# First block's output projection inside the mixer's last steps, and the gate of the linear attention on ScalarE

## What is computed

```python
def _gla_output(o, g, norm_g):
    ...                                     # o: linear attention, normalised per head
    return (...).astype(o.dtype) * jax.nn.silu(g)

def _trunk_layer(x, cvec, lp, ctx, pos):
    sh1, sc1, gt1, sh2, sc2, gt2 = jnp.split(jax.nn.silu(cvec) @ w_ada + b_ada, 6, axis=-1)
    h = _rmsnorm(x, n1) * (1 + sc1) + sh1
    ...                                     # h @ w_in, split among three mixers: pool, GLA, attention
    mix = jnp.concatenate([y_pool, y_gla, y_attn], axis=-1)
    x = x + gt1 * (mix @ w_out)             # output projection, gated residual
    h2 = _rmsnorm(x, n2) * (1 + sc2) + sh2
    x = x + gt2 * _peer(h2, peer_wq, peer_subkeys, peer_u, peer_v)
```

## Time and profile before

| | us |
|---|---|
| median of 3 runs | 4006.52 |
| the profiled execution's own time | 3995.5 |
| its span, first to last instruction | 3993.7 |
| TensorE busy | 3697.8 |
| VectorE busy | 2609.3 |
| GpSimd busy | 1616.5 |
| ScalarE busy | 680.5 |
| mean granted clock of TensorE | 0.961 |

### The profile page before, as it was taken

The page is one execution under the profiler, slowest core; times in us unless marked ns, Lnnn a source line. Parts: engine busy times, 40 slices in busy tenths (PEclk is TensorE's granted clock), DMA queues, the critical chain, the costliest instruction groups (busy, mean ns, idle before and its releaser), DMA issues. The chain is left out here.

```text
span 3993.7 us, 40043 instructions
## 1 busy us (share of the span) xinstructions
PE 3697.8 (93%) x13766; PEld 2139.0 (54%) x13766; DVE 2609.3 (65%) x5973; ACT 680.5 (17%) x1534; POOL 1616.5 (40%) x1498
## 2 busy tenths in 40 slices
PE   2988978999999999999979888889999999999997
PEld 1556676655555555554445666766555555555543
DVE  5786588776666666677724738978677646566444
ACT  1031356500000000000012224652000000000000
POOL 0030055445566544444402002553677655444330
PEclk7987999999999999999989799999999999999998
DMA  6321134579999999999930131447899999989783
GB/s 222 122 95 50 74 96 138 158 291 406 374 380 374 377 372 378 376 377 355 372 129 2 44 117 38 133 138 254 340 410 410 390 364 344 367 338 359 290 308 130
DMA packets 364809, 1026.96 MB, mean 257 GB/s; under 512 B 30784, under 2 KB 132416, under 8 KB 363840
## 3 DMA queue, kind: packets, MB, share of 16 engines
q0 software_dynamic: 147456, 536.94, 35.1%
q1 hardware_dynamic: 117424, 433.99, 28.5%
q10 hardware_dynamic: 99728, 53.48, 4.8%
HBM read 965.07 MB, written 59.22 MB: 256 GB/s over the span
## 5 line engine op out<-in xcount | busy, mean ns | idle before, releaser
L1835 PE MATMUL ps<-colsT,arena 128*128 128x384 f32 x4096 | 1358.7, 486 | 4.2 <-DMA arena<-in_peer_ut 4.2
L1835 PEld LDWEIGHTS ps<-colsT,arena 128*128 128x128 f32 x4096 | 775.9, 190 | 582.6 <-issue 94.7
L1870 PE MATMUL ps<-arena 128*128 128x512 f32 x1536 | 676.4, 592 | 0.0
L1349 POOL DMA_INDIRECT proj<-in_peer_u,eidx x336 | 460.0, 1369 | 244.0 <-DVE modbc L1541 116.1
L1349 POOL DMA_INDIRECT proj<-in_peer_v,eidx x335 | 359.5, 1073 | 315.7 <-DVE colsT L1552 216.9
L1870 PEld LDWEIGHTS ps<-arena 128*128 128x128 f32 x1536 | 291.8, 190 | 345.2 <-issue 317.6
L1335 POOL TENSOR_SCALAR x<-iota,modbc 128x128 f32<-128x128 f32 x192 | 145.0, 770 | 759.9 <-ACT modbc L1672 593.0
L1541 DVE CUSTOM_DVE_ANT_0 proj<-proj,rows 128x1024 f32<-128x1024 f32 x336 | 400.4, 1224 | 56.3 <-DMA proj<-in_peer_u,eidx 54.6
L1552 DVE SCALAR_TENSOR_TENSOR colsT<-proj,modbc,colsT 128x1024 f32<-128x1024 f32 x330 | 409.6, 1285 | 14.9 <-DMA proj<-in_peer_v,eidx 14.7
L1870 PE MATMUL ps<-arena,rows 128*128 128x512 f32 x768 | 337.8, 592 | 0.0
L1870 PE MATMUL ps<-arena,x 128*128 128x512 f32 x768 | 337.8, 592 | 0.0
(11 more groups left out here) (295 smaller groups left out, 3775.2 us busy)
## 6 DMA issues: line engine op xcount, KB each, us to landing
arena<-in_peer_ut SPq DMA_DIRECT2D x256, 512.0 KB, 6.7
arena<-in_peer_v SPq DMA_DIRECT2D x256, 512.0 KB, 6.7
gmat_d<-arena ACTq DMA_DIRECT2D x24, 2048.0 KB, 9.3
arena<-gmat_d SPq DMA_DIRECT2D x64, 768.0 KB, 8.7
proj<-in_w_adaT SPq DMA_DIRECT2D x48, 512.0 KB, 9.2
modbc<-in_w_adaT SPq DMA_DIRECT2D x30, 512.0 KB, 3.7
rows<-in_w_adaT SPq DMA_DIRECT2D x18, 512.0 KB, 3.5
arena<-in_w_in SPq DMA_DIRECT2D x2, 4224.0 KB, 17.4
```

The costliest lines, as they stand in the source:

```text
L1349: pool.indirect_dma_start(ring[slots[at]], None, tab, bass.IndirectOffsetOnAxis(ap=eidx[:, b * SLOTS + q:b * SLOTS + q + 1], axis=0)).then ...
L1835: mm = pe.matmul(ps[:, 2 + j % 2, 0:ND], utab[:, j % UR, k], hT[:, k, NG:T], start=(k == 0), stop=(k == KT - 1))
L1870: mm = pe.matmul(ps[:, Y_BANKS[2 * d + c2], :], wT[j % CR][:, d * P:(d + 1) * P], vtab[:, j % VR, c2 * 512:(c2 + 1) * 512], start=(j == 0) ...
```

## The change

Four things, in both layers.

1. The gate. ScalarE now makes the whole of 1/(1+exp(-g)) in step 11, as exp(-ln(1+exp(-g))): three passes over 128x1280 (Exp, Ln, Exp). VectorE's add and reciprocal of step 12 are gone, and its wait for `sg_ready` stands in step 13.
2. The projection. `out_proj(0)` moves into the mixer block as `first_projection`: its first half stands in step 21 behind `turn_y(18)`, its second in step 22 behind `turn_y(19)`. It writes PSUM banks 6 and 7 in place of 0 and 1. The first half waits for w_out, for the copies of `gt1` on ScalarE and VectorE, and for the attention output of its token block.
3. The gate row. The first DMA of the second block is the latents' gate row alone (0.5 MB, to `loaded`). SP waits for it to land before it issues `w_q`; behind `w_q` stand the prompt's gate row (0.5 MB) and shift and scale for both kinds (2 MB), which only the residuals of blocks 0 and 1 wait for (`rows_landed`).
4. `residual(0)` waits for no matmul of the second block, since the barrier stands between; `residual(i)` waits for `wo_mm` at i.

```diff
--- before.py
+++ after.py
@@ -191,8 +191,7 @@
         sem("av_done"), sem("y_made"), sem("yt_done"), sem("yt_sb"), sem("es_ready"), sem("gs_half"), sem("gs_done"))
     go_done, P_ready, gla_ready, gm_ready, gy_ready, sg_ready, pool_d = (
         sem("go_done"), sem("P_ready"), sem("gla_ready"), sem("gm_ready"), sem("gy_ready"), sem("sg_ready"), sem("pool_d"))
-    wq_landed = (
-        sem("wq_landed"))
+    wq_landed, rows_landed = sem("wq_landed"), sem("rows_landed")
     sc_half, ms_made, root_made = sem("sc_half"), sem("ms_made"), sem("root_made")
     dots_ready, gelu_ready, coef_ready = sem("dots_ready"), sem("gelu_ready"), sem("coef_ready")
 
@@ -766,6 +765,18 @@
                         turn_mod()
                     else:
                         turn_gla(n)
+
+                def first_projection(n):
+                    if n == 0:
+                        pe.wait_ge(wo_landed, 16)
+                        pe.wait_ge(u_act, ACT_AT["gt1"])
+                        pe.wait_ge(u_dve, DVE_AT["gt1"])
+                        pe.wait_ge(y_moved, 1)
+                        pe.wait_ge(yt_sb, pairs_.index((3, DB[0])) + 1)
+                    b = DB[0]
+                    for k in range(KT):
+                        pe.matmul(ps[:, 6 + n, :], mixT[:, k, b * P:(b + 1) * P], w_out[:, k, n * 512:(n + 1) * 512],
+                                  start=(k == 0), stop=(k == KT - 1))
 
                 if l > 0:
                     turn_normed(pe)
@@ -814,6 +825,8 @@
                         state_mm(2)
                     if SC0_STEP <= s < SC0_STEP + NB:
                         chunk_out(s - SC0_STEP)
+                    if s >= PSTEPS - 2:
+                        first_projection(s - PSTEPS + 2)
 
             @block.scalar
             def _(act):
@@ -891,8 +904,10 @@
                         act.wait_ge(yt_sb, NB)
                         act.activation(mixT[:, 4, :], ytmp, ACT.Copy).then_inc(y_moved, 1)
                     if s == 11:
-                        act.activation(sg.rearrange("p b c -> p (b c)"), gg.rearrange("p b c -> p (b c)"), ACT.Exp,
-                                       scale=-1.0).then_inc(sg_ready, 1)
+                        flat = lambda q: q.rearrange("p b c -> p (b c)")
+                        c.link(act.activation(flat(sg), flat(gg), ACT.Exp, scale=-1.0))
+                        c.link(act.activation(flat(sg), flat(sg), ACT.Ln, bias=1.0))
+                        act.activation(flat(sg), flat(sg), ACT.Exp, scale=-1.0).then_inc(sg_ready, 1)
                     if s == OUT_STEP:
                         act_rstd(act, c, None, gm_ready, gy_ready, msg, yg, zg)
 
@@ -1059,11 +1074,8 @@
                             c.done(dve.tensor_tensor(v(arr)[:, :, 32:64], v(arr)[:, :, 32:64], v(right)[:, :, 32:64], ALU.mult))
                         c.wait()
                         dve.sem_inc(qk_ready, 1)
-                    if s == 12:
+                    if s == 13:
                         dve.wait_ge(sg_ready, 1)
-                        c.link(dve.tensor_scalar(f(sg), f(sg), 1.0, None, ALU.add))
-                        c.link(dve.reciprocal(f(sg), f(sg)))
-                    if s == 13:
                         c.link(dve.tensor_tensor(f(sg), f(sg), f(gg), ALU.mult))
                         c.link(dve.tensor_tensor(sg, sg, gnorm.unsqueeze(1).to_broadcast([P, NB, 256]), ALU.mult))
                     if s == OUT_STEP:
@@ -1158,7 +1170,7 @@
         R2 = 2 * PH
         WO = (2, 3, 4, 0, 1)
         QUNITS = [(b, 1, 4 * i, 4, 2 + i) for b in DB for i in range(2)] + [(0, 2, 2 * i, 2, 2 + i % 2) for i in range(4)]
-        OP_BANKS = (0, 2, 0, 0, 2)
+        OP_BANKS = (6, 2, 0, 0, 2)
         TR_BANKS = (4, 2, 2, 2, 2)
         HT_COUNT = (KT, 2 * KT, 3 * KT, 3 * KT + 2, 3 * KT + 4)
         NQ = len(QUNITS)
@@ -1272,6 +1284,10 @@
                     dst = modbc[:, :].rearrange("p (v n) -> p v n", v=2)[:, :, dst_m * D:(dst_m + n) * D]
                     return sp.dma_start(dst, src)
 
+                def gate_row(v):
+                    src = bass.AP(tensor=modrow_d.tensor, offset=(l * 12 + v * 6 + 2) * D, ap=[[0, P], [1, D]])
+                    return sp.dma_start(mb[:, v, G1], src)
+
                 def load_ada(n):
                     if n >= NMOD:
                         return
@@ -1279,8 +1295,11 @@
                         sp.wait_ge(ada_used, n - 1)
                     sp.dma_start(late_ada[n % 2], a["w_adaT"][l + 1, n]).then_inc(w_landed[n % 2], 16)
 
-                mod_rows(G1, 2, 3).then_inc(loaded, 16)
+                gate_row(1).then_inc(loaded, 16)
+                sp.wait_ge(loaded, 16)
                 sp.dma_start(w_q, a["w_q"][l].rearrange("(k p) n -> p k n", p=P)).then_inc(wq_landed, 16)
+                gate_row(0).then_inc(rows_landed, 16)
+                mod_rows(SH2, 3, 2).then_inc(rows_landed, 16)
                 sp.dma_start(xb[:, 0:DB[0]], (a["x"] if l == 0 else xs_d)[0:DB[0]].rearrange("b p d -> p b d")).then_inc(x_landed, 16)
                 sp.dma_start(skT, a["skT"][l]).then_inc(sk_landed, 16)
                 for i, b in enumerate(DB):
@@ -1360,7 +1379,9 @@
                         dve.wait_ge(loaded, 16)
                     if b in GB:
                         dve.wait_ge(x_landed, 16)
-                    dve.wait_ge(wo_mm, i + 1)
+                        dve.wait_ge(rows_landed, 32)
+                    if i > 0:
+                        dve.wait_ge(wo_mm, i)
                     bank = OP_BANKS[i]
                     c.link(dve.tensor_tensor(rb[:, b], ps[:, bank:bank + 2, :].rearrange("p a n -> p (a n)"), mb[:, v, G1], ALU.mult))
                     dve.tensor_tensor(xb[:, b], xb[:, b], rb[:, b], ALU.add).then_inc(x_ready, 1)
@@ -1881,7 +1902,6 @@
                     elif (k, step) == (2, 0):
                         query(9)
 
-                out_proj(0)
                 out_proj(1)
                 turn_rows(0)
                 out_proj(2, (0,))
```

## The result

The kernel after takes 3970.99 us (median; 3968.92 to 3978.11), the kernel before 4006.89 us in the same comparison. The ratio is 0.9914, 95% interval 0.9896 to 0.9931: 0.9% faster, 35.9 us by the medians. The forecast was 3985 (3971 to 3999), so the time fell on the very edge of the range. A second set of runs of the same kernel, beside other experiments, gave 3972.13 us, ratio 0.9915 (0.9899 to 0.9931). The profiled execution of after has a span of 3971.1 us, the one of before had 3993.7: 22.6 us apart, which is less than the 35.9 of the medians. Of the 43 executions of before timed beside the experiments one took 4138.5 us at a mean clock of 0.916, and it stands outside the ratios and the spreads given here.

What follows compares the result with a forecast made beforehand. TensorE, busy 93% of the span, bounds the kernel, so gains come only where it stands still or runs at half clock. Terms 8.4 + 2 + 0.45 = 10.85 us a layer, 21.7 in all, take 4006.5 to 3985 us (range 3971 to 3999).

Steps and rivals of the forecast that it cites:

- Gate off VectorE: Steps 12 and 13: without VectorE's 9.04 us of gate work, the first chunk_copy comes 8.4 us earlier a layer.
- ScalarE at no cost: Step 11: Ln, Exp and two table loads, 5.1 us, fit ScalarE's wait with 3.0 us of room left.
- The clock: Four steps behind the first chunk_copy: short half-clock stretches replace the long one, gaining 2 us a layer.
- S: Length of four steps, first chunk_copy to fifth, 40.87 us before; forecast to gain 2 us a layer by the clock.
- rival A: Clock stays high through all four steps behind the first chunk_copy: 3970 us; 16 in 100.
- rival B: Clock stays low through all four steps behind the first chunk_copy: 4004 us, no change that can be told; 9 in 100.
- D: Length from fifth chunk_copy to query(0): drain, projection, first rows; only the projection's 0.45 us a layer was forecast there.
- The projection: Where the blocks meet: half a projection covers the wait for turn_y(19) and ScalarE's last copy, gaining 0.45 us a layer.
- up to 3.5 us of a slow start: Start of the moved projection: a clock still slow there costs up to 3.5 us, put into the range only.
- Row and w_q free: Head of second block: row takes 3.3 us, w_q 13.1; free by 2.2 us at turn_rows(0), 4.7 at query(0).
- From the profiled execution to the median: Whole kernel: the 21.7 us gain, found in the profiled execution, was subtracted unchanged from the median, 4006.5 to 3984.8.

Runs made afterwards that it cites:

- gate_only: Kernel before with only the gate edit (its three passes on ScalarE, VectorE's add and reciprocal gone): 3977.72 us, ratio 0.9931.
- busy_step19: Kernel after with 32 MATMULs that nothing reads filling TensorE's 7.57 us wait in step 19: 3963.03 us, ratio 0.9896.
- gate_and_busy_step19: Kernel before with only the gate edit, plus 32 unused MATMULs in step 19's wait: 3971.19 us, ratio 0.9913.
- one_row_load: Kernel after with gate row, shift and scale for both token kinds loaded at once ahead of w_q, as before: 3983.55 us, ratio 0.9947.
- the later multiplies: Kernel after with VectorE's two gate multiplies moved from step 13 to steps 14 and 15: 3975.43 us, ratio 0.9919.

## Why the prediction was right, and where it was off

*Gate off VectorE, 8.4 us a layer:* right; 8.45, with the new wait of 0.52 us on VectorE and 3.31 us on TensorE, both as written.

*ScalarE at no cost:* right; 6.4 us of passes, 2.81 us of room left.

*The clock, +2 us a layer:* this is the term that was mis-sized. S came out at 34.74 us, so it gave 6.1 us a layer and not 2. I had argued that most of the four steps had run at the slow clock and so would go on to. In fact one stretch of some 10 us took the place of one of 36: the first step is slow (11.54 us) and the other three are not. It is not rival A either, which had all four at full clock, 31.5 us. Two readings behind this term were off. In the trace of before the clock had already fallen 0.6 us into the wait of 6.25, so the wait stood ahead of the slow steps, but its length was not what lowered the clock. And rival B's "three of the steps were so" does not fit the steps of before, of which two were slow (12.12, 11.44), one half so (9.43) and one fast (7.88). The sentence I weighed from the Trainium skill ("TensorE: Matmul & The Clock Gate", Part 1), that the slow clock is the default and sustained work releases it, would have made the term zero or negative. In S it did not hold as I had read it: the work between the chunks is as small as before and the clock came back. In D it fits in part: in gate_only the clock came back 5.0 and 4.6 us into the 64 dense MATMULs and in layer 1 of after 0.8 us into the dense ones, but in layer 0 of after it was back before any of them.

*What I did not look at:* D. The wait of 7.56 us in step 19 is in the trace of before, and I had not asked what the shorter chain would do to the clock behind it. With the gate edit alone D rises by 4.3 us, which takes back most of the 6.1. The net clock gain of gate_only, 1.8 a layer, is near my 2 by luck: it is the difference of two larger terms, of which I had named one.

*The projection, 0.45 us a layer:* right as a direct saving. From `turn_y(18)` to the query it is 37.91 us before (387.26 to 425.17) and 37.36 after (373.65 to 411.01), 0.55. Alone it moved the time by nothing that its interval can tell, ratio 0.9993. But on top of the gate edit the time fell by 6.7 us, most of it by the clock. I had put this interaction (up to 3.5 us of a slow start) into the range with the remark that as much would fall on the work in its place before. That was the weak step: work in front of the barrier and work behind it are not alike for the clock, as busy_step19 and gate_and_busy_step19 show (1.00 against 0.72 around it).

*Row and w_q free:* right; 3.8 and 13.0 us, with 1.7 and 4.7 us of room, and one_row_load shows what the row order is worth: 12.6 us.

*From the profiled execution to the median:* this step was wrong. I subtracted the same number from both. The forecast gain was 21.7 us, the spans of the two traces are 22.6 apart, the medians 35.9. In the traces the sum came out near, in part by luck: S gained 12.2 us where 4 were forecast, D lost 1.1 where 0.9 of gain were forecast, and 1.2 and 4.0 us were lost between the layers and behind layer 1's first query, for which there was no term. The other 13.3 us had no term at all: the profiled execution of before (3995.5 us) lies 11.4 under its median and that of after 1.9 over its own. That the time still touches the range is luck.

The timed executions of before spread from 3995.7 to 4012.0 (42 beside the experiments, 8 of them under 4000), and the mean granted clock of each is on record. Of the eight under 4000 us seven have 0.960 or 0.961 and one 0.967; of the 19 over 4007 us fifteen have 0.956 or 0.957 and four 0.962 or 0.963. Within either group of clocks the longer executions have 0.004 less. Over some 4000 us that is 32 us more at half clock, which costs up to 16 us, an estimate from these numbers, and it covers the spread. So before has executions some 10 us slower than the one profiled, with more of the half clock in them, and they make up most of the 13.3. Where in the program it lies is not shown: S varied from 34.6 to 44.9 in kernels of nearly the same code there, but no execution was profiled at the slow end of before.

*Open:* what decides when the clock comes back in the four steps. With the 6.25 us wait filled, S was 39.3 and 34.6 in one execution; with the 3.31 us wait gone, 38.8 and 44.8, 38.9 and 36.3, and 44.9 and 36.3; with that wait in place, 34.7 or 34.8 sixteen times out of sixteen (eight profiled executions of seven kernels, two layers each). Open too is why in layer 0 of after the clock came back before the projection, and in gate_only did not. The wait of 3.31 us seems to make the length steady, and I have no run that says why.

## What to carry over

When work is taken off the engine that TensorE waits for, count the shorter wait, and then follow the granted clock to the next long wait and through the one behind it: here the clock gave 6.1 us and took back 4.3 beside the gate edit's direct 8.4, and it was several times the direct 0.55 of the projection. In this kernel the wait of TensorE just ahead of the drain and the projection was the place for independent MATMULs, even for a part of the projection, and the barrier was better crossed with dense work on its near side. Check an edit that only moves a wait by its timed runs and by more than one profile: the later multiplies removed 3 us of waiting a layer and alone gained nothing that can be told. And take the spread of the kernel's own executions into the range before a difference of two profiles is carried over to the medians.

## What was not expected of the hardware

- TensorE busy for 43.54 of 45 us with small matmuls (32x64 to 128x256) ran at a mean granted clock of 0.62, so a full busy row is no sign of a high clock.
- Filling a wait of 6.25 us with 28 MATMULs gained nothing (4006.3 us against 4006.7); filling one of 7.57 us with 32 gained 8.0 us. What follows differs (small matmuls with waits of 1.27 and 2.94 us in the first case), but that this is the cause was not tried.
- After a wait of only 0.39 us and a barrier of 1.63 us, with small matmuls around them, 64 MATMULs took 29.20 us in place of 27.70 (30.76 in the other layer, with a wait of 0.69 us).
- The reciprocal over 128x1280 took 8.15 us on VectorE, while each pass of ScalarE over the same tile took 1.27 us and each table load 1.28 us.
